# Two feed-forward blocks of a decoder trunk by one level of Strassen's scheme, with the sums of weights on GpSimd

## The reference, cut to what matters

```python
def swiglu(h, w_gu, w_d):
    gu = h @ w_gu
    return (jax.nn.silu(gu[..., :D_FF]) * gu[..., D_FF:]) @ w_d
...
        hp = hp + swiglu(rms_norm(hp, norm_ffn[layer]), w_gate_up[layer], w_down[layer])
        hs = hs + swiglu(rms_norm(hs, norm_ffn[layer]), w_gate_up[layer], w_down[layer])
    y_prompt = rms_norm(hp, norm_final)
    y_sample = rms_norm(hs, norm_final)
```

## Time and profile before

| what | us |
|---|---|
| median of three runs | 1306.17 |
| span of the profiled execution | 1304.2 |
| feed-forward block of layer 0, one unbroken stretch of PE (from 211.78) | 354.01 |
| "gu" within it, 212 to 448: PE, DVE, ACT, POOL busy | 236.00, 78.18, 71.70, 57.52 |
| "dn" within it, 448 to 566: PE, DVE, ACT, POOL busy | 118.00, 36.96, 29.20, 11.75 |

### The profile page before, as it was taken

One profiled execution on the slowest core, in us unless ns is written; L12 is line 12 of the kernel. 1 busy time (PEld: TensorE's weight loads), 2 busy tenths in 40 slices (PEclk: granted clock), 3 DMA queues, 4 the chain that ended last, 5 costly groups with the idle time before them and its releaser, 6 DMA issues.

```text
span 1304.2 us, 27642 instructions
## 1 busy us (share of the span) xinstructions
PE 1285.2 (99%) x11347; PEld 1077.4 (83%) x11347; DVE 640.4 (49%) x1038; ACT 501.9 (38%) x809; POOL 374.7 (29%) x584
## 2 busy tenths in 40 slices
PE   8999999999999999999999999999999999999997
PEld 6767588888888888888888888887888888888886
DVE  6456644333333333357887787776632333332232
ACT  6233544223232322236565565654532222222321
POOL 1004313222222101047554545552312121211100
PEclk9999999999999999999999999999999999999999
DMA  8658522242223322220213222132222223233211
GB/s 263 221 168 289 167 98 97 98 159 96 96 96 109 133 90 89 74 88 34 73 58 98 75 88 82 50 98 91 105 97 96 99 94 102 91 124 130 90 45 66
DMA packets 32139, 140.88 MB, mean 108 GB/s; under 512 B 4633, under 2 KB 6937, under 8 KB 20154
## 3 DMA queue, kind: packets, MB, share of 16 engines
q1 hardware_dynamic: 32058, 139.75, 31.5%
HBM read 128.63 MB, written 11.11 MB: 107 GB/s over the span
## 4 chain that ended last, share of the span: by engine, by line
PE 91%; DVE 5%; ACT 2%; issue 1%; POOL 0%; DMA 0%; SPq 0%; DVEq 0%; POOLq 0%
PE P L1780 64%; PE P L2138 10%; PE P L2327 2%; PE P L2313 1%; PE P L2388 1%; PE P L2147 1%; PE P L1858 1%; PE P L2321 1%; DVE wl L1524 1%; PE P L2357 1%; PE P L2153 1%; PE P L1990 1%; PE P L2368 1%; PE P L2339 1%; PE P L1933 1%
## 5 line engine op out<-in xcount | busy, mean ns | idle before, releaser
L1780 PE MATMUL P<-zh,wh 128*128 128x260 f16 x1712 | 329.3, 273 | 2.4 <-DVE wl L1229 2.4
L1780 PE MATMUL P<-zl,wh 128*128 128x260 f16 x1712 | 329.2, 273 | 0.0
L1780 PE MATMUL P<-zh,wl 128*128 128x260 f16 x1712 | 329.1, 273 | 0.0
L1209 DVE SCALAR_TENSOR_TENSOR wl<-stage,wh 128x2048 f16<-128x2048 f32 (+1 forms) x75 | 185.3, 2471 | 195.3 <-ACT wh L793 192.8
L1780 PE MATMUL P<-arena,wh 128*128 128x260 f16 x1816 | 276.2, 274 | 0.9 <-DVE hT L1424 0.3
L1780 PEld LDWEIGHTS P<-arena,wh 128*128 128x128 f16 x1816 | 175.7, 97 | 28.6 <-issue 1.2
L1780 PEld LDWEIGHTS P<-zh,wh 128*128 128x128 f16 x1712 | 164.3, 97 | 34.2 <-issue 8.1
L1780 PEld LDWEIGHTS P<-zh,wl 128*128 128x128 f16 x1712 | 165.7, 97 | 25.7
L1780 PEld LDWEIGHTS P<-zl,wh 128*128 128x128 f16 x1712 | 165.5, 97 | 25.7
L1780 PE MATMUL P<-arena,wl 128*128 128x260 f16 x908 | 174.6, 273 | 0.0
L793 ACT ACTIVATE wh<-stage 128x2048 f16<-128x2048 f32 (+1 forms) x80 | 161.8, 2023 | 3.6 <-PE P L1780 3.6
(11 more groups left out here) (378 smaller groups left out, 1645.1 us busy)
## 6 DMA issues: line engine op xcount, KB each, us to landing
stage<-w_gu SPq DMA_DIRECT2D x44, 1024.0 KB, 4.9
stage<-w_in SPq DMA_DIRECT2D x23, 1024.0 KB, 5.0
stage<-w_dn SPq DMA_DIRECT2D x16, 1408.0 KB, 6.0
arena<-cache_k SPq DMA_DIRECT2D x32, 256.0 KB, 3.4
stage<-w_out SPq DMA_DIRECT2D x8, 1024.0 KB, 5.4
arena<-cache_v SPq DMA_DIRECT2D x32, 256.0 KB, 3.0
arena<-delta_state SPq DMA_DIRECT2D x8, 512.0 KB, 3.7
o_ds<-arena SPq DMA_DIRECT2D x8, 512.0 KB, 6.9
```

What stands on the lines that cost most here:

```text
L1209: nc.vector.scalar_tensor_tensor(out=wl[:, j, 0:words], in0=stage[:, j, 0:words], scalar=WS, in1=wh[:, j, 0:words], op0=MUL, op1=SUB).then ...
L1780: mm = nc.tensor.matmul(pm[j][:, c, :], w[:, wslot, o:o + 128], x[:, k, c * CH:(c + 1) * CH], start=(k == first and w is wh and x is xh), ...
```

## The change

Both feed-forward blocks are computed by seven block products in place of eight (Winograd's form of Strassen's scheme). The two halves of the tokens, the two halves of k and a pair of column blocks (256 gate and 256 up features, or two tiles of the down matrix) make a 2 by 2 block problem. There are 19 such units, 11 of gate and up and 8 of down. Each unit has seven weight blocks of 1024 words per partition in gate and up, 768 or 640 in down: three as loaded (B11, B21, B22) and four that POOL makes by additions, T1 = B12 + B11, T2 = T1 + B22, T3 = B12 + B22 and T4 = T2 + B21 (signs are taken into the activations). ACT and DVE split all seven blocks into high and low parts, in a ring of five. The activations get sums of their own: three on POOL behind the product of gate and up, whose low parts are now made on DVE. PE adds several products in one bank of PSUM; DVE and ACT take quarters of 260 columns out of it.

```diff
+NG, NU = 11, 19
+KINDS = ("B11", "T3", "T2", "B21", "T1", "T4", "B22")
+RING = [m % 5 for m in range(NB7 - 7)] + [2, 3, 4, 2, 3, 4, 2]
...
+# GpSimd
+            def weight_sum(kind, n, layer):
...
+                elif kind == "T2":
+                    pool.wait_ge(t_sum, len(SUMS) * layer + SUM_AT["T1", n])
...
+                        pool.wait_ge(c_lo, base + 7 * (n - 1) + (7 if n == 13 else 6))
+                    a, b = source("T1", n), source("B22", n)
+                else:
+                    pool.wait_ge(t_sum, len(SUMS) * layer + SUM_AT["T2", n])
+                    pool.wait_ge(ld3, 16 * (NU * layer + n + 1))
+                    pool.wait_ge(c_lo, base + 7 * n + 3)
+                    a, b = source("T2", n), source("B21", n)
+                nc.gpsimd.tensor_tensor(source(kind, n), a, b, ADD).then_inc(t_sum, 1)
+            def gated(n, layer):
+                nc.gpsimd.tensor_tensor(g, g, u, MUL).then_inc(prod_done, 1)
...
+            def ffn(layer):
...
+                for n in range(NU):
+                    if 1 <= n <= NG:
+                        gated(n - 1, layer)
+                    weight_sum("T2", n + 1, layer)
+                    weight_sum("T3", n + 2, layer)
+                    weight_sum("T1", n + 2, layer)
+                    weight_sum("T4", n + 1, layer)
...
+# ScalarE, unit n, product i
+                        if NEXT[k]:
+                            act.wait_ge(f_mm, done(layer, k))
+                        for m in NEXT[k]:
+                            convert(m, layer)
...
+                        if 1 <= n <= NG and i == 3:
+                            x, p = quad(gts[(n - 1) % 2]), n - 1
+                            act.wait_ge(prod_done, 4 * (NG * layer + n - 1) + 4)
+                            nc.scalar.activation(fxh[:, 0, p, :], x[:, 0, :], ACT.Copy, scale=-1.0)
...
+# VectorE
+            def convert(m, layer):
...
+                dve.wait_ge(c_hi, NB7 * layer + m + 1)
+                nc.vector.scalar_tensor_tensor(out=ringl[:, o:o + w], in0=source(KINDS[i], n), scalar=WS,
+                                               in1=ringh[:, o:o + w], op0=MUL, op1=SUB).then_inc(c_lo, 1)
...
+                for n in range(NU):
+                    for i in range(7):
+                        if n < NG and i >= 3:
+                            finals(n, i)
+                        if n >= NG:
+                            leave_quarter(n, i)
+                        for m in NEXT[7 * n + i]:
+                            convert(m, layer)
+                        if 1 <= n <= NG and i in (3, 4):
+                            low_parts(n - 1, i == 4)
...
+            def low_parts(p, second):
...
+                        dve.wait_ge(f_hi, NG * layer + p + 1)
+                        nc.vector.scalar_tensor_tensor(out=fxl[:, 0, p, :], in0=x[:, 0, :], scalar=-1.0,
+                                                       in1=fxh[:, 0, p, :], op0=MUL, op1=SUB)
+                        nc.vector.tensor_tensor(fxl[:, 1:3, p, :], x[:, 2:4, :], fxh[:, 1:3, p, :], SUB)
...
+            def half_operands(layer, at):
...
+                        link(nc.vector.tensor_tensor(s[:, 0, :], ztile[:, p, CH:T], zb[:, CH:T], SUB))
+                        link(nc.vector.tensor_tensor(s[:, 1, :], ztile[:, p, 0:CH], s[:, 0, :], SUB))
+                        nc.vector.tensor_tensor(s[:, 2, :], zb[:, 0:CH], s[:, 1, :], SUB).then_inc(z_s, 1)
+                        dve.wait_ge(z_hi, KD * b + seen)
+                        nc.vector.tensor_tensor(zfs[1][:, 1:3, p, :], quad(zb), zfs[0][:, 1:3, p, :], SUB)
+                        nc.vector.tensor_tensor(zxs[1][:, :, p, :], s, zxs[0][:, :, p, :], SUB).then_inc(z_lo, 1)
...
+# TensorE
+                        m = 7 * n + i
+                        pe.wait_ge(c_lo, NB7 * layer + m + 1)
...
+                            for k in range(a, z):
...
+                                for w, x in ((ringh, xh), (ringh, xl), (ringl, xh)):
+                                    mm = nc.tensor.matmul(bank, w[:, o:o + 128], x[:, k, :],
...
+            ffn(0)
+            pe.wait_ge(dn_out, LEAVES)
             unit("in1", 0, 0, zh, zl, z_ready(2), lambda: statistics(2))
```

More of the change, by code:

```diff
@@ L39 @@
 OUT_ROWS = (3, 4, 2, 0, 1, 5, 6, 7)
+FFN_ROWS = (tuple(range(8)), OUT_ROWS)
 NPG = PAST // PAGE
@@ L60, with k_range, block_words, product_count @@
 UNITS = _u
+NG, NU = 11, 19
+KINDS = ("B11", "T3", "T2", "B21", "T1", "T4", "B22")
+OPERAND = (0, 3, 5, 1, 4, 2, 6)
+NB7 = 7 * NU
+RING = [m % 5 for m in range(NB7 - 7)] + [2, 3, 4, 2, 3, 4, 2]
+PREV = [max((i for i in range(m) if RING[i] == RING[m]), default=None) for m in range(NB7)]
+NEXT = {k: [m for m in range(NB7) if PREV[m] == k] for k in range(NB7)}
+PRODUCTS, FINALS, LEAVES, COPIES = 14 * NG + 7 * (NU - NG), 10 * NG, 7 * (NU - NG), 6 * NG
+SUMS = [("T3", 0), ("T1", 0), ("T2", 0), ("T3", 1), ("T1", 1), ("T4", 0)]
+for _n in range(NU):
+    SUMS += [(k, i) for k, i in (("T2", _n + 1), ("T3", _n + 2), ("T1", _n + 2), ("T4", _n + 1)) if i < NU]
+SUM_AT = {s: i + 1 for i, s in enumerate(SUMS)}
+def k_range(n):
+    return (0, 4) if n < NG else ((0, 6), (6, 11))[(n - NG) % 2]
+def block_words(n):
+    return 1024 if n < NG else 128 * (k_range(n)[1] - k_range(n)[0])
+def product_count(m):
+    n, i = divmod(m, 7)
+    return 14 * n + 2 * i + 2 if n < NG else 14 * NG + 7 * (n - NG) + i + 1
+def halves(rows):
+    events, come = [], []
+    for k in rows:
+        come.append(k)
+        new = [("A", k)] if k < 4 else []
+        p = k % 4
+        if p in come and p + 4 in come:
+            new.append(("B", p))
+        events.append(new)
+    return events
 LEVELS = 6
@@ L458, in _, with ffn_load @@
[L458 to L461, removed]
+            def ffn_load(kind, n, layer):
+                p = n % 2
+                i, j = int(kind[1]) - 1, int(kind[2]) - 1
+                dst = source(kind, n)
+                if n < NG:
+                    src = w_gu[layer][2 * n + j][:, 1024 * i:1024 * i + 1024]
+                else:
+                    a, b = k_range(n)
+                    src = w_dn[layer][2 * ((n - NG) // 2) + j].rearrange("p (k two c) -> p two k c", two=2, c=128)[
+                        :, i, a:b, :]
+                    dst = dst.rearrange("p (k c) -> p k c", c=128)
+                sp.dma_start(dst, src).then_inc(ld3 if kind == "B21" else ld2[p] if kind == "B22" else ld1[p], 16)
```

729 lines of the change are left out of this document (470 added, 259 removed).

## The result

The changed kernel takes **1456.12 us** (median of 4 runs, 1455.04 to 1458.73) against 1306.16: ratio 1.1151, 95% interval 1.1135 to 1.1167. It is slower, as forecast, but by 150 us and not by 42, and lies above the range of 1262 to 1425.

The account below looks back on a forecast made before the run. PE's matmul count bounds each block before; after, DVE and POOL's contest bounds gate and up. Per block 265 + 105 = 370 in place of 354, +32 for two, edges +10: 1306.2 + 32 + 10 = 1348 us, range 1262 to 1425.

Parts of the forecast that it names:

- Mechanism and sign: In gate and up, contest between DVE and POOL replaces PE as the bound; the kernel gets slower, chance 0.77.
- the 23 to 26 us announced: Sign that the forecast is right: a gate unit takes 23 to 26 us, against 18.8 if wrong.
- PE's term: Per block, 2772 matmuls at 0.1117 us: 206.5 us for gate and up, 103.2 for down, 309.7 in place of 354.0.
- That PE would wait for `wl`: Sign that the forecast is right: in gate and up, PE waits for DVE's low parts of weights.
- "+3 each, +6 for two": Entering each block, the last tile's chain and three block splits end at about 8.5 us; two products (5.4) cover part.
- "265, the mean of the two counted contests": Gate and up of a block: 301 us of joint DVE and POOL work over 1.136 gives 265, against 236.0 before.
- The factor 1.136: Joint DVE and POOL work done per microsecond of contest, from two counted places in the trace: 8.04 / 7.08.
- the prediction's own lines: Durations alone by length: DVE 0.15 us fixed plus 1.046 ns a word, POOL 0.19 us plus 2.11 ns.
- The bounds of 1.04 to 1.16: Range of the contest factor: gate and up 289 us at 1.04, 259 at 1.16; kernel 1410 or 1329 us.
- "I take 105": Down of a block: 114 to 120 us of joint work over 1.136 gives 100 to 105, beside PE's 103.2.
- full exclusion: Rival: DVE and POOL never overlap, 301 and 117 us per block, 1444 us; 15% jointly with worse, chain and clock.
- A granted clock under 1.00: Sign against the forecast, in gate and up; the clock rival put the kernel past 1634 us, within a shared 15%.

Follow-up runs that it names:

- the micro kernel: A separate kernel that only sets DVE and POOL against each other: eight low parts and eight additions of 1024 took 26.24 us together, 9.17 and 18.41 alone.
- the memsets: Against the changed kernel, each of POOL's sums of weights replaced by two memsets of the same tile, which read nothing: 1292.63 us.
- the early load: Against the changed kernel, weight block B22 of unit 1 loaded early into a free part of the arena, not after the statistics: 1447.84 us.

## Why the prediction was wrong

**Mechanism and sign: right.** DVE and POOL, each hidden alone, don't run side by side, and their joint time replaces PE's. Low parts and sums became long, PSUM reads did not, DVE was busy throughout, a gate unit fell into the 23 to 26 us announced; the micro kernel, the memsets and the sums on VectorE each show it by itself. PE's term, 0.1117 us a matmul, held within 0.6 us a unit once POOL's sums stopped reading (19.39 for 18.8). That PE would wait for `wl` was wrong but for 4.0 us: it waited for PSUM reads behind low parts.

**The step that failed most: "+3 each, +6 for two", the edges into a block.** To the end of the first gate unit +28.6 and +36.2 us were measured, where 5.6 was forecast for each block (3 for the edge, 2.6 for the unit). The prediction counted the last tile's chain at durations alone, from the moment at which PE is done with it, and let two products hide most of it. But DVE's order left the last out tile of block 0 at 216.18 us, where it had left it at 205.57 before. POOL's sums and the operands' subtractions contend here already: such a subtraction takes 0.43 us elsewhere, and 2.46 beside a sum (DVE, then POOL):

```profile
198.49 2.46 DVE L1695 TENSOR_TENSOR arena<-arena 128x260 f32<-128x260 f32 x1 [0.80 <-ACT arena L1015]
...
198.31 2.35 POOL L736 TENSOR_TENSOR arena<-stage,arena 128x1024 f32<-128x1024 f32 x1
```

Left out, too, were that POOL's order sets T3 and T1 of the next unit, with a load, ahead of T4 (4.1 us a block by the early load); that PE's statistics wait for squares (6.5 us); and that the granted clock over the first unit, with PE idle for 20 of its 51 us, was 0.77. With sums that read nothing the start of block 0 is still 18.2 us longer than before; the seven products in down alone, with none of this at the start, add 1.3 us up to the end of gate and up. DVE's order, changed alone where the sums were on VectorE, gave back 1.3 us in block 0 and none in block 1. The cause of 10.1 of the 28.6 us in block 0, and of what block 1 has beyond them, stays open.

**"265, the mean of the two counted contests".** Steady units took 25.7 us in place of 24.1 (the last two are shorter). The factor 1.136 came mostly from instructions of 512 and 520 elements; what a pair saves is a fixed 0.17 us, 0.29 against the prediction's own lines, so longer instructions give a smaller factor: 1.051 for 1024, and 27.3 / 25.7 = 1.06 in the unit. The bounds of 1.04 to 1.16 held, the centre did not.

**"I take 105" for down.** 123.1 in block 0. The prediction divided the joint work by f and found it level with PE, as if the two queues always had something to run beside each other. Without the sums' reads 103.4 were measured with the same waits for loads, so the reads are needed for the loss; but DVE was busy 94.33 and POOL 76.94 of 123.09, not full, so here the contest acts through waits: a sum that waits for its load and then takes longer, and a quarter that stands behind a long low part. How much each of the two adds was not separated.

**Of the rivals** full exclusion (1444) came nearest in time, but not by its reason: eleven units at 25.7 are 282 us, not its 301, and the starts, which no case had priced, made up for it. A granted clock under 1.00, which the prediction named as a sign against it, did appear, 0.90 in the steady unit and 0.94 in down. It did not set the steady unit, where DVE was busy for 25.57 of 25.70 us, and it was 1.00 there as soon as the sums' reads were gone; what it cost in the starts was not separated.

## What to carry to other kernels

Before giving GpSimd work to "free" VectorE, add up VectorE's instructions with two SBUF inputs and GpSimd's instructions that read SBUF as if one engine did them, less 0.2 to 0.3 us a pair, and hold that against the bound; if the sum doesn't fit, the work is cheaper on VectorE itself (a sum of 1024 takes 1.15 us there and 2.30 on GpSimd). Measure a contest factor at the lengths that it will be used for, and price the start of a block by all that stands ahead in each engine's order, not by the durations of one tile's chain. A scheme that trades matmuls for sums pays only in the stretch where the sums' engines have room: here in down, 1% of the kernel.

## What was not expected of the hardware

Low parts beside a GpSimd copy with a single input took 15.04 us for eight, against 9.17 alone: one SBUF input on GpSimd is enough. Beside additions of only 260 elements eight low parts of 1024 took 12.92, and eight of these additions 13.43, about one of each in turn, as if the short instruction waited for the long one as a whole.
